# A two-block network on one core: the attention of the first block in double steps

## What is computed

```python
k, v = concat(k_ctx, k_lat), concat(v_ctx, v_lat)      # 768 keys, 8 heads
q = (rmsnorm(zq, g_q) @ w_q_b) ; q[..., 64:] = rope(...)  # 96 wide
logits = einsum('bqhd,bkhd->bhqk', q_block, k) / sqrt(96)
p = softmax(logits)
o = einsum('bhqk,bkhd->bqhd', p, v)                    # 64 wide
# layer 0 does the same for 256 context queries over the 256 context keys
merged = concat(rmsnorm(attn), rmsnorm(conf), rmsnorm(sc)) @ w_o
```

## Time and profile before

| | |
|---|---|
| median of the runs | 3640.69 us |
| the profiled execution | 3641.39 us |
| its span | 3640.1 us |
| TensorE busy | 96% of the span |
| VectorE busy | 59% |
| ScalarE busy | 39% |
| attention of layer 0 | about 181 to 397 us |
| attention of layer 1 | about 1166 to 1333 us |

### The profile page before, as it was taken

One profiled execution on the slowest core, in us unless ns is written; L12 is line 12 of the kernel. 1 busy time (PEld: TensorE's weight loads), 2 busy tenths in 40 slices (PEclk: granted clock), 3 DMA queues, 4 the chain that ended last, 5 costly groups with the idle time before them and its releaser, 6 DMA issues.

```text
span 3640.1 us, 49724 instructions
## 1 busy us (share of the span) xinstructions
PE 3486.0 (96%) x20631; PEld 2931.8 (81%) x20631; DVE 2165.2 (59%) x3627; ACT 1429.4 (39%) x2269; POOL 464.7 (13%) x427
## 2 busy tenths in 40 slices
PE   7999999999989999999999999999989999999999
PEld 5855778888877567888777777799989999988889
DVE  3276563333364856444645535389999987766666
ACT  3245532221233464222344533333566573333332
POOL 0000000000000000000000111003332443343330
PEclk9999999999999999999998999999999999999999
DMA  6400112333212002222321243257777898999994
GB/s 247 162 20 1 59 59 104 116 117 127 105 47 84 1 31 76 103 93 99 115 76 47 96 138 128 83 182 270 263 267 258 288 351 318 353 333 342 330 332 171
DMA packets 123666, 581.56 MB, mean 160 GB/s; under 512 B 14080, under 2 KB 31600, under 8 KB 82480
## 3 DMA queue, kind: packets, MB, share of 16 engines
q1 hardware_dynamic: 67744, 365.46, 28.0%
q0 software_dynamic: 55696, 212.91, 16.4%
HBM read 516.97 MB, written 61.34 MB: 159 GB/s over the span
## 4 chain that ended last, share of the span: by engine, by line
PE 75%; DVE 16%; ACT 4%; DMA 2%; issue 2%; POOL 1%; SPq 0%; DVEq 0%; ACTq 0%; POOLq 0%
PE ps L675 20%; PE ps L676 20%; PE ps L677 20%; DVE WL L546 2%; PE ps L3299 2%; PE ps L1429 2%; DVE ACC L1631 2%; DVE UB L3116 1%; DVE OH L3016 1%; PE ps L578 1%; DVE MX L1604 1%; PE ps L2946 1%; PE ps L1508 1%; PE ps L758 1%; PE ps L1447 1%
## 5 line engine op out<-in xcount | busy, mean ns | idle before, releaser
L546 DVE TENSOR_TENSOR WL<-stage,WH 128x2048 fp32r<-128x2048 f32 x239 | 546.1, 2285 | 333.0 <-ACT WH L536 307.1
L675 PE MATMUL ps<-HH,WH 128*128 128x512 f32 (+1 forms) x1672 | 619.0, 370 | 22.2 <-DVE HL L1001 16.8
L676 PE MATMUL ps<-HL,WH 128*128 128x512 f32 (+1 forms) x1672 | 610.3, 365 | 0.0
L677 PE MATMUL ps<-HH,WL 128*128 128x512 f32 (+1 forms) x1672 | 607.4, 363 | 0.0
L536 ACT ACTIVATE WH<-stage 128x2048 fp32r<-128x2048 f32 x239 | 455.0, 1904 | 386.5 <-PE ps L677 329.6
L675 PEld LDWEIGHTS ps<-HH,WH 128*128 128x128 f32 x1672 | 318.2, 190 | 87.9 <-issue 31.1
L675 PE MATMUL ps<-HP,WH 128*128 128x384 f32 (+1 forms) x1088 | 375.8, 345 | 9.7 <-DVE WL L546 8.7
L677 PE MATMUL ps<-HP,WL 128*128 128x384 f32 (+1 forms) x1088 | 369.5, 340 | 0.0
L676 PE MATMUL ps<-LP,WH 128*128 128x384 f32 (+1 forms) x1088 | 369.5, 340 | 0.0
L677 PEld LDWEIGHTS ps<-HH,WL 128*128 128x128 f32 x1672 | 317.1, 190 | 51.8
L676 PEld LDWEIGHTS ps<-HL,WH 128*128 128x128 f32 x1672 | 318.2, 190 | 49.1 <-issue 1.2
(11 more groups left out here) (478 smaller groups left out, 5576.6 us busy)
## 6 DMA issues: line engine op xcount, KB each, us to landing
stage<-in_w SPq DMA_DIRECT2D x64, 1024.0 KB
stage<-in_u SPq DMA_DIRECT2D x64, 1024.0 KB
stage<-in_v SPq DMA_DIRECT2D x64, 1024.0 KB
stage<-in_w_mod SPq DMA_DIRECT2D x40, 1024.0 KB
adram<-GA SPq DMA_DIRECT2D x128, 192.0 KB
GR<-gdram POOLq DMA_DIRECT2D x32, 768.0 KB
AR<-adram POOLq DMA_DIRECT2D x32, 768.0 KB
gdram<-GST SPq DMA_DIRECT2D x20, 1024.0 KB, 8.9
```

The costliest lines, as they stand in the source:

```text
L546: dve.e.tensor_tensor(k.WL[o % 2][:, 0:w], k.stage[n % 2][:, 0:w], k.WH[o % 2][:, 0:w].bitcast(F32), ALU.subtract).then_inc(*dve.done("sla ...
L675: pe.e.matmul(o, wh[:, kk, cs], L.view(L.hh, kk, z), start=first, stop=False)
L676: pe.e.matmul(o, wh[:, kk, cs], L.view(L.hl, kk, z), start=False, stop=False)
L677: mm = pe.e.matmul(o, wl[:, kk, cs], L.view(L.hh, kk, z), start=False, stop=last)
```

## The change

`att_order` now steps by two units, in both layers. `old` are the two units of the step before, `scored` the two new ones. A step yields: turn of the first old one, scores of the first new one, a head part, an item of `behind`; turn of the second old one, **exp of the first new one**, scores of the second new one, a head part, an item; exp of the second new one; the pair, if one is due; values of the first old one, one or two items; values of the second old one, one or two items; the scaling of the pair. `exp` is an event of its own, which only ScalarE acts on; the maximum on VectorE stays at `scores`. `out` stands at the start of the step, and a pair is due in the same step as the `out` of its second head. The squares of the outputs (`att_sq`) come after all units.

```diff
-    scored, turned, outs, pairs, head, done = [], [], [], [], [], 0
+    scored, outs, head, done = [], [], [], 0
...
-    for n, u in enumerate(units + [None, None, None]):
-        ended = pairs.pop(0) if pairs else None
+    more = 1 if l == 0 else 2
+    for n in range(0, len(units) + 2, 2):
+        old, scored, ended = scored, units[n:n + 2], None
         if outs:
             out = outs.pop(0)
             yield "out", out
-            if out % 2 == 1:
-                pairs.append(out // 2)
-        if u is not None:
-            yield "scores", u
-            scored.append(u)
-            if n % per == per - 4 and u[0] + 1 < 8:
-                head = [(u[0] + 1, part) for part in range(3)]
-        if head:
-            yield "head", head.pop(0)
-        if behind:
-            yield "behind", behind.pop(0)
+            if out % 2 == 1 and out < 7:
+                ended = out // 2
+        for i in range(2):
+            if old:
+                yield "turn", old[i]
+            if i == 1 and scored:
+                yield "exp", scored[0]
+            if scored:
+                yield "scores", scored[i]
+                if (n + i) % per == per - 4 and scored[i][0] + 1 < 8:
+                    head = [(scored[i][0] + 1, part) for part in range(3)]
+            if head:
+                yield "head", head.pop(0)
+            if behind:
+                yield "behind", behind.pop(0)
+        if scored:
+            yield "exp", scored[1]
         if ended is not None:
             yield "pair", ended
-        if len(scored) > 2 or (u is None and scored):
-            yield "turn", scored[0]
-            turned.append(scored.pop(0))
-        if len(turned) > 1 or (u is None and turned):
-            v = turned.pop(0)
-            yield "values", v
-            if v[1] == units[-1][1]:
-                outs.append(v[0])
+        for i in range(2):
+            if old:
+                yield "values", old[i]
+            for _ in range(more):
+                if behind:
+                    yield "behind", behind.pop(0)
+        if old and old[1][1] == units[-1][1]:
+            outs.append(old[1][0])
         if ended is not None:
             yield "scaled", ended
-        for _ in range(1 if l == 0 else 2):
-            if behind:
-                yield "behind", behind.pop(0)
-        if u is None and not behind:
-            yield "att_sq", done
-            done += 1
...
-        elif kind == "scores":
+        elif kind == "exp":
             n = att_count(l) * u[0] + u[1] // 128
             pb = k.Pb.take(act, (l, u), ("turned", (l, u)))
             act.wait_ge("row_max", (l, u))
```

## The result

The changed kernel takes 3655.61 us (median of 6 runs, 3651.83 to 3661.56) against 3640.30 of the kernel before (6 runs): ratio 1.0043, 95% interval [1.0033, 1.0053], +15.3 us. Forecast were 3652 and a range of 3638 to 3663. The profiled execution took 3651.83 us, span 3650.5, +10.4 on that of before.

A forecast was written before the change was run, and what follows sets the result against it. TensorE, busy 96% of the span, was taken as the bound. The profiled 3641.4 us plus 7.5 (layer 1) and 4 (layer 0) gave 3652.9, or 3652 on the median's scale, range 3638 to 3663.

The forecast's parts named there:

- Fewer switches: TensorE, both layers: 40 fewer visits to column tiles at 0.33 us each, saving 13 us of its work.
- Rival D: Saving of a switch is nil, two adjacent values take 1.62 us; up to 9 us more, 3661; chance 0.1.
- The stall at S.1 of layer 1: Second new unit's scores wait for the first's exp, queued behind a copy on ScalarE; 1.97 us once a head.
- kh to kh: Layer 1, between successive heads' kh products without a pair: 17.64 us after the change, 16.55 before.
- The pair: Layer 1: scores wait for the pair's scaling behind VectorE's taps, 1.7 us more on top of the pair's own 1.8.
- The layer 1 term: Attention of layer 1: new waits for exp and scaling outweigh saved switches, +7.5 us.
- rival C: New stalls bring TensorE's half clock, 4 us in each of 7 heads, +28, 3680 us; chance 0.05.
- Rival B: No change to tell: later stalls absorb half the waits, layer 1 +4, layer 0 0, 3645 us; chance 0.25.
- Layer 0: Attention of layer 0: start +2.1, four heads -0.2, remainder +2.0, together +4 us.
- The start: Start of layer 0's attention: rope of head 1 comes at 213.2 instead of 211.1 us, +2.1.
- The four heads: Layer 0 heads paced by a three-engine loop: 20.9 us for 21.3, 23.6 for 23.3 with a pair; -0.2 in all.
- Rival A: Exps come early enough; switches saved and today's stalls lost, 10 us in layer 1, 3 in layer 0: 3628; chance 0.1.

The follow-up runs named there:

- e9: e5 with the values of the first old unit ahead of the second's turn in layer 1, so no two values adjoin; 3636.4 us, 0.9987 of the kernel before.
- e1: Changed kernel with each exp right behind its scores on ScalarE, ahead of the copies; 3644.8 us, 1.0009 of the kernel before.
- e3: Changed kernel with the new order in layer 0 only, the old order in layer 1; 3647.1 us, 1.0018 of the kernel before.
- e10: Changed kernel with layer 1 as in e5, and layer 0's exp right behind its scores except for units 0 and 1 of a head; 3629.8 us, 0.9965.
- e2: Changed kernel with the new order in layer 1 only, the old order in layer 0; 3654.0 us, 1.0034 of the kernel before.
- e5: Changed kernel with layer 0 in old order; in layer 1 exp behind its scores, scaling right behind the pair, taps spread 3, 5, 0, 4; 3633.3 us, 0.9978.
- e7: Changed kernel with the head parts kh, qh and rot one unit later in layer 1; 3659.9 us, 1.0044 of the kernel before.
- e5 again: The kernel of e5 unchanged, timed once more beside e9 and e10; 3631.9 us, 0.9976 of the kernel before.

## Why the prediction was right

The number lies within the range, and the waits on which the forecast rests were found at their places and at nearly their lengths. In part it is luck: a gain in the tail that was counted too small and a clock that was taken as full cancel in layer 1, and in layer 0 the parts of the sum are off in both directions.

- *Fewer switches.* The estimate was 0.33 us a visit; e9 gives 0.31, and two V in a row take 1.46 us. Rival D is out. The number of visits was 40 in the forecast; in the timelines it falls from 36 to 19 in layer 1 and from 52 to 26 in layer 0, 43 fewer.
- *The stall at S.1 of layer 1.* Forecast 1.97 us; it is 1.81 in five heads, 2.40 in head 2 and 1.95 in the last. *The stall at the values*, forecast 0.56: 0.49. *kh to kh*, forecast 17.64: 17.52. The mechanism is the one described, with one thing too few: the copy on ScalarE is not alone. The late maximum holds the same S.1 for 1.95 us by itself (e1). The prediction saw the lag of VectorE and found it just covered, which it is as long as exp is late anyhow.
- *The pair.* The wait for the scaling, forecast 1.7, is 1.07 and 1.61. From kh of head 2 to kh of head 7 it is 100.0 us (1197.13 to 1297.14) against the 97.8 predicted; without the 3.4 us that its products at half clock take longer it is 96.6.
- *The layer 1 term*, forecast +7.5; measured +10.2 in the stage. It is two terms. The order costs 5.0 us at full clock, 2.5 less than forecast. Half of the 2.5 is in heads 2 to 6 (96.6 for 97.8, mostly the 0.12 a head and the pairs). The other half is behind kh of head 7, where I counted a gain of 1.4 and took the tail as equal: it is 50.1 us for 50.9 before, and about 48.5 without the half clock. The clock costs some 5.
- *The clock*, rival C. I gave it 0.05, at 4 us for each of seven heads, 28 in all. It happened in part, behind three of the seven waits at S.1, at about 1.7 us each. My forecast had a granted clock of 1.00 throughout layer 1; this is the term that was wrongly put at nothing. With the 2.5 us above on the other side it leaves the median 3.6 us above the forecast. The row that I set against it, a stage at 1.00 with stalls of 0.47, has no stall of the size in question. The trace of before had such ones that I did not use, 2.27 us at the stage's start and 2.55 at 1305.58, and both were followed by full clock; e3 shows that the second one is no proof. The section "A second HAM failure mode: psum-queue depth-cycling" of the page "TensorE: Matmul & The Clock Gate" in the Trainium skill tells of a bf16 kernel in which short pauses between groups that cycle through PSUM make the clock swing; by it C would have been the likeliest. The trace agrees in part: waits of 1.8 to 2.4 us for a PSUM tile were followed by half clock in three cases of seven.
- *Rival B*, stalls of which later ones absorb half, is out: kh follows kh at the full 17.52 us in layer 1, and layer 0 is longer too.
- *Layer 0*, forecast +4: +4.6, +2.8 and +3.8 in three executions, e3 +6.5 by runs. The single waits are well met: the stall at S.5, 1.52: 1.36; at qh, 0.68: 0.52; around silu, 5.8: 5.7 (2.00 + 1.31 + 2.38). The loop, 20.9 and 23.6, is 20.74 and 23.45. The parts of the sum are not. The start, +2.1, is +0.7, and -0.2 but for a wait for weights ahead of it that is 0.9 us longer than before (1.96 for 1.06): the first scores ran at full clock this time (1.00 over 194 to 202 us, where the earlier trace rows has 0.57). The four heads, -0.2, are +1.0, because two pairs fall between rot of head 1 and rot of head 5 where it was one. The rest, +2.0, is +2.9 though it has a pair less: two waits of 1.78 and 1.81 us stand ahead of S in heads 6 and 7 (317.11, 343.48), which I had not counted, the first with half clock behind it. So the +4 is right as a sum and partly by luck.
- *Rival A*, 3628, has not come true, since the exps do come too late. e10 comes near its number, 3630, only with further edits, and by other parts: 7.0 us in layer 1 where A has 10, and 4.2 in layer 0 where it has 3.

Not settled: what decides whether a wait of about 2 us brings the half clock. In layer 1 it came behind some of them in each profile that has the late exp or the late maximum, at times behind the 2.26 us at the stage's start (e2, e5, e7), once behind 1.60 (e2), and in e3 behind the old order's 2.55. It did not come in the layer 1 stages of before, e9, e10 and e5 again, though each of them begins with the same 2.26 or 2.27 us. The same instructions with the same wait had it in one execution and not in another (1.78 us in layer 0 of the changed kernel, 2.55 in layer 1 of before and e3, 2.26 in e5 and e5 again). No experiment set the length of a wait by itself.

## What to carry to other kernels

When two steps of a pipeline are joined, write down for each engine what its queue holds between an input's arrival and its use, and for a ring of tiles who the taker after next is: here each joined step put a copy ahead of an exp, and a ring of three free tiles turned that into a wait of TensorE. Look for a second wait under the first before its removal is priced: with the cause of one of two waits of 2 us gone the stage of layer 1 at full clock went from 171 to 165 or 168 us (most of the 168 by a third wait, in the pairs), with all three to 159, where the old order had 166. What an order saves on the engine that bounds (0.3 us a switch) is kept only if the engines that feed it are re-spread in the same edit.

## What the runs showed of the hardware

- One visit of the pair of column tiles, in and out, costs 0.31 us of TensorE (e9 against e5 again, 4.6 us of busy time for 15 visits), and two such groups in a row take 1.46 us where two apart take 1.62.
- TensorE fell to 1.2 GHz behind single idle stretches of 1.60 (e2), 1.81 and 2.40 us (the changed kernel), with TensorE busy 86% of the stage. The mean granted clock of the layer 1 stage was 0.94 to 0.97 in the kernels with waits of about 2 us in several heads and 0.99 to 1.00 in those without them there. A single wait does not decide it: 2.55 us before the same product was followed by a granted clock of 1.00 in the kernel before and of 0.77 in e3, and in e9 1.88 us in the tail and 2.26 at the start passed at 1.00.
- One such fall cost about 1.7 us in the changed kernel (three in layer 1, some 5 us of 176.5).
